# A hybrid decoder step on one core: a fixed expert in the last block, row reads ahead of the last scatter, and a product moved to GpSimd

## The reference

```python
s = sigmoid(h @ w_router)                    # 64 scores, 4 of 8 groups kept
eidx = top_k(masked s + b_router, 8)         # 8 experts of a token
wts = s[eidx] / sum(s[eidx]) * 2.5
routed = sum over the 8 experts e of wts * ((silu(h @ we_g[e]) * (h @ we_u[e])) @ we_d[e])
yf = routed + (silu(h @ ws_g) * (h @ ws_u)) @ ws_d
x = x + gt2 * rms_norm(yf, g_ffn_post)
```

## Time and profile before

| | |
|---|---|
| median of three runs | 1107.8 us (1106.04 to 1108.03) |
| profiled execution | 1108.23 us |
| its span, first to last instruction | 1106.4 us |
| granted TensorE clock, mean | 0.992 |
| busy: TensorE, VectorE, ScalarE, GpSimd | 1065.5, 729.2, 215.3, 136.3 us |
| bytes moved, mean rate | 337.11 MB, 305 GB/s |

### The profile page before, as it was taken

The page is one execution under the profiler, slowest core; times in us unless marked ns, Lnnn a source line. Parts: engine busy times, 40 slices in busy tenths (PEclk is TensorE's granted clock), DMA queues, the critical chain, the costliest instruction groups (busy, mean ns, idle before and its releaser), DMA issues.

```text
span 1106.4 us, 16559 instructions
## 1 busy us (share of the span) xinstructions
PE 1065.5 (96%) x5954; PEld 535.9 (48%) x5954; DVE 729.2 (66%) x1934; ACT 215.3 (19%) x473; POOL 136.3 (12%) x163
## 2 busy tenths in 40 slices
PE   6999999999999999999999999999899999999797
PEld 3456678777877644664333333333233333333242
DVE  3218441546546645766988888888687987888148
ACT  4131332222233313301111111111011110111111
POOL 0110000000020010111121211111112111121100
PEclk9999999999999999999999999999999999999999
DMA  9958720120352277769999999999999999999798
GB/s 368 339 197 301 244 81 24 53 86 1 115 190 87 77 242 248 293 283 380 409 413 425 424 425 424 422 424 427 422 425 424 423 424 420 412 416 406 255 425 334
DMA packets 51653, 337.11 MB, mean 305 GB/s; under 512 B 9636, under 2 KB 14088, under 8 KB 30830
## 3 DMA queue, kind: packets, MB, share of 16 engines
q1 hardware_dynamic: 33710, 287.32, 64.2%
q0 software_dynamic: 17856, 48.68, 11.6%
HBM read 311.30 MB, written 37.24 MB: 315 GB/s over the span
## 4 chain that ended last, share of the span: by engine, by line
PE 79%; DMA 12%; DVE 5%; ACT 2%; issue 1%; SPq 0%; DVEq 0%; ACTq 0%
PE bank L1594 23%; PE bank L1617 12%; PE bank L1289 10%; DMA mem<-in_w_exp_down 6%; PE bank L1308 5%; PE bank L1407 3%; DMA hT<-in_w_exp_down 3%; PE bank L1408 3%; PE bank L1525 3%; PE bank L1202 3%; PE bank L1286 3%; DMA mem<-in_w_sh_down 2%; PE bank L1703 2%; PE bank L1177 1%; DVE mem L2290 1%
## 5 line engine op out<-in xcount | busy, mean ns | idle before, releaser
L1594 PE MATMUL bank<-mem 128*32 128x512 f32 (+2 forms) x1568 | 334.0, 595 | 1.8 <-DVE mem L2290 1.0
L2290 DVE STREAM_TRANSPOSE mem<-mem 32x256 f32<-32x256 f32 x448 | 195.1, 436 | 5.8
L1617 PE MATMUL bank<-mem 128*32 128x512 f32 (+2 forms) x712 | 178.4, 608 | 10.9 <-DMA mem<-in_w_exp_down 7.0
L1594 PEld LDWEIGHTS bank<-mem 128*32 128x32 f32 (+2 forms) x1568 | 106.9, 128 | 164.9 <-issue 164.9
L1289 PE MATMUL bank<-hT,mem 128*128 128x288 f32 x512 | 133.3, 409 | 1.0 <-ACT mem L968 1.0
L2290 DVE STREAM_TRANSPOSE mem<-x_sb 32x256 f32<-32x256 f32 x240 | 104.5, 435 | 3.1
L1289 PEld LDWEIGHTS bank<-hT,mem 128*128 128x128 f32 x512 | 93.8, 190 | 25.8 <-issue 2.4
L1617 PEld LDWEIGHTS bank<-mem 128*32 128x32 f32 (+2 forms) x712 | 56.8, 133 | 81.4 <-issue 71.1
L1594 PE MATMUL bank<-x_sb,mem 128*32 128x512 f32 (+2 forms) x256 | 87.1, 596 | 0.0
L2306 DVE COPY hT<-bank 128x512 f32<-128x512 f32 x48 | 33.1, 691 | 67.2 <-PE bank L1617 67.1
L822 POOL DMA_INDIRECT mem<-ffn_in_rows,idxg x32 | 32.9, 1030 | 268.0 <-DVE idxs L2274 192.6
(11 more groups left out here) (404 smaller groups left out, 1218.9 us busy)
## 6 DMA issues: line engine op xcount, KB each, us to landing
mem<-k_w_exp SPq DMA_DIRECT2D x54, 2048.0 KB
mem<-in_w_exp_down SPq DMA_DIRECT2D x52, 1024.0 KB
x_sb<-k_w_exp SPq DMA_DIRECT2D x10, 2048.0 KB
mem<-k_w_ada SPq DMA_DIRECT2D x8, 2048.0 KB, 9.2
mem<-k_w_in SPq DMA_DIRECT2D x7, 2048.0 KB, 9.0
hT<-in_w_exp_down SPq DMA_DIRECT2D x12, 1024.0 KB
mem<-expert_out_rows SPq DMA_DIRECT2D x6, 2048.0 KB, 15.7
mem<-k_w_head SPq DMA_DIRECT2D x4, 2048.0 KB, 17.3
```

The source lines that it names most:

```text
L1594: i = mm(bank[sl, :], xT[:, j % 2, c * BLK + sl.start:c * BLK + sl.stop], gu_view(r)[:, c, :], start=c == 0, stop=c == KC - 1)
L1617: i = mm(ps[4 + hf][sl, :], hhT[:, k * BLK + sl.start:k * BLK + sl.stop], dn_view(r)[:, k, hf * 512:(hf + 1) * 512], start=k == 0, stop=k ...
L2290: i = dve.transpose(cols[dl, :, sl], rows[sl, :, dl])
```

## The change

Three things are changed together.

1. Expert 63 always takes rank 63, and rank 63 has a block of its own, the last one (capacity 128 rows). `CAPS` is in another order for it, of the same 48 blocks, and the fourth preloaded expert goes to rank 24 instead of 5. Expert 63 is the highest number, so its rows are slot 7 alone; slots 0 to 6 are complete once the scatter before the last has landed.
2. SyncE loads the shared down weights ahead of the x rows. Once the last gate-up product is done and all scatters but the last have landed, it reads the sample tile's slots 0 to 3 and slots 0 to 3 of token tiles 0 and 1 (buffers 0, 1 and 3). The sample tile's slots 4 to 7 and the rest follow the last scatter. Row sets are renumbered, as the sample tile is one set now, and a buffer is free again when VectorE and, for the first set of a tile, TensorE have used it.
3. TensorE adds three instead of four rows of tiles 0, 1 and 2, VectorE five instead of four. The product with the weight row moves to GpSimd for all tiles but the last, and VectorE waits for it (`pch`). VectorE's order becomes own_sum 0, own_sum 1, add_sums 0, residual 0, add_sums 1, then for each further tile own_sum, the residual of the tile before, add_sums.

In the overflow path, which does not run here, the early sets are read a second time.

```diff
-PRE = [0, 1, 4, 5]
+PRE = [0, 1, 4, 24]
+CAPS = [4, 4, 2, 2, 4, 3, 2, 3, 3, 5, 2, 2, 3, 3, 6, 2, 2, 4, 2, 2,
+        4, 2, 2, 5, 4, 3, 4, 4, 4, 2, 2, 3, 1, 3, 5, 3, 1, 3, 3, 3, 3, 5, 6, 1, 4, 4, 4, 2,
+        2, 3, 3, 3, 3, 4, 2, 2, 2, 3, 3, 2, 2, 2, 2, 4]
...
-        COMBINE = [(NCH, KPE)] + [(t, KPE) for t in range(NCH - 1)] + [(NCH - 1, KPE // 2)]
+        COMBINE = [(NCH, KPE)] + [(t, KPE - 1) for t in range(NCH - 1)] + [(NCH - 1, KPE // 2)]
...
+            sp.wait_ge(S["eup"], last_use(EXTSLOT) + 1)
+            load_down(sp, dn_s, A["w_sh_down"][0], S["ld_br"])
             sp.wait_ge(S["eup"], last_use(XSLOT) + 1)
             sp.wait_ge(S["xT_ready"], NBK)
             for t in range(NT):
                 sp.dma_start(x_sb[0:ROWS[t], t, :], x1_d[t * P:t * P + ROWS[t], :]).then_inc(S[f"ld_x{t}"], 16)
-            sp.wait_ge(S["eup"], last_use(EXTSLOT) + 1)
-            load_down(sp, dn_s, A["w_sh_down"][0], S["ld_br"])
+            EARLY = [1, 3]
+            sp.wait_ge(S["eup"], NBK)
+            sp.wait_ge(S["sct0"], 16 * (NBK // 2))
+            sp.wait_ge(S["sct1"], 16 * (NBK // 2 - 1))
+            y_sample(0, "yh0")
+            for q in EARLY:
+                y_rows(q, COMBINE[(q + 1) // 2][0], 0, KPE, f"yh{q}")
...
             for k in range(2):
                 sp.wait_ge(S[f"sct{k}"], 16 * (NBK // 2))
-            for k in range(2):
-                sp.dma_start(yhalf[k:P:2, 0, :], yv[SEQ:T, KPE * k * D:KPE * (k + 1) * D]).then_inc(S[f"yh{k}"], 16)
+            y_sample(1, "yh6")
...
+                    if q >= NYH:
+                        sp.wait_ge(S["yd_sum"], (q - NYH + 1) // 2 + 1)
+                        if (q - NYH) % 2:
+                            sp.wait_ge(S["yp_mm"], (q - NYH + 1) // 2 + 1)
...
+            for i in range(LAST):
+                t = COMBINE[i][0]
+                n = ROWS[t]
+                pool.wait_ge(S["yl_sum"], i + 1)
+                if i:
+                    pool.wait_ge(S["x2_done"], i)
+                pool.tensor_tensor(tgain[0:n], yo[0:n, i % 2, :], bcG[0:n, int(t == NCH), :], ALU.mult).then_inc(S["pch"], 1)
...
-                    y = rows(q, n, 0, KPE)
+                    dve.wait_ge(S[f"yh{(q - 1) % NYH}"], ycount(q - 1))
+                    y = rows(q - 1, n, kp, KPE) + rows(q, n, 0, KPE)
...
-                tt_(tgain[0:n], yo[0:n, i % 2, :], bcG[0:n, o, :], ALU.mult)
+                if i < LAST:
+                    dve.wait_ge(S["pch"], 3 + i)
+                else:
+                    tt_(tgain[0:n], yo[0:n, i % 2, :], bcG[0:n, o, :], ALU.mult)
...
-            for i in range(NT):
+            own_sum(0)
+            own_sum(1)
+            add_sums(0)
+            residual(0)
+            add_sums(1)
+            for i in range(2, NT):
                 own_sum(i)
+                if i < LAST:
+                    residual(i - 1)
                 add_sums(i)
-                if i != LAST - 1:
-                    residual(i)
+            residual(LAST)
```

More of the change, by code:

```diff
@@ L73 @@
 LASTB = [max(b for b in range(NBK) if any(s[2] == r for s in SEGS[b])) for r in range(len(CAPS))]
-RANK = [PRE.index(r) if r in PRE else 0 for r in range(len(CAPS))]
-for i_, r_ in enumerate(sorted((r for r in range(len(CAPS)) if r not in PRE), key=lambda r: -CAPS[r])):
+RANK = [PRE.index(r) if r in PRE else 0 for r in range(len(CAPS) - 1)] + [len(CAPS) - 1]
+assert LASTB.count(NBK - 1) == 1 and CAPS[-1] * QS == BLK
+for i_, r_ in enumerate(sorted((r for r in range(len(CAPS) - 1) if r not in PRE), key=lambda r: -CAPS[r])):
     RANK[r_] = len(PRE) + i_
@@ L680, in _, with y_rows, y_sample @@
                 sp.dma_start(x_sb[0:ROWS[t], t, :], x1_d[t * P:t * P + ROWS[t], :]).then_inc(S[f"ld_x{t}"], 16)
-            sp.wait_ge(S["eup"], last_use(EXTSLOT) + 1)
-            load_down(sp, dn_s, A["w_sh_down"][0], S["ld_br"])
+            yv = y_d.rearrange("(t k) d -> t (k d)", k=TOPK)
+            def y_rows(q, t, k0, k1, s):
+                at_ = (k0 - (q + 1) % 2 * KPE) * D
+                sp.dma_start(yhalf[0:ROWS[t], q % NYH, at_:at_ + (k1 - k0) * D], yv[t * P:t * P + ROWS[t], k0 * D:k1 * D]).then_inc(S[s], 16)
+            def y_sample(k, s):
+                sp.dma_start(yhalf[k:P:2, 0, :], yv[SEQ:T, KPE * k * D:KPE * (k + 1) * D]).then_inc(S[s], 16)
+            EARLY = [1, 3]
+            assert DN_PLACE[NE - 1] not in (1, 3)
+            sp.wait_ge(S["eup"], NBK)
[4 more added lines that the diff above has]
+                y_rows(q, COMBINE[(q + 1) // 2][0], 0, KPE, f"yh{q}")
             nov = overflow_count(sp)
@@ L691, in body, with early_landed @@
                 load_dn(NE + j, e)
+            def early_landed():
+                for q in [0] + EARLY:
+                    sp.wait_ge(S[f"yh{q}"], 16)
             def last_rows():
@@ L697, in last_rows @@
                 sp.sem_inc(S["over"], 1)
-            overflow(sp, nov, body, last=last_rows)
+                y_sample(0, "ld_br")
+                for q in EARLY:
+                    y_rows(q, COMBINE[(q + 1) // 2][0], 0, KPE, "ld_br")
+            overflow(sp, nov, body, early_landed, last_rows)
             sp.wait_ge(S["xT_ready"], NBK)
@@ L721, in _ @@
                         y_rows(q, t, KPE // 2, KPE, f"yh{q % NYH}")
[L722 to L724 removed]
+            y_rows(2 * LAST, t, KPE, TOPK - 2, f"yh{2 * LAST % NYH}")
+            y_rows(2 * LAST, t, TOPK - 2, TOPK - 1, "yh5")
+            y_rows(2 * LAST, t, TOPK - 1, TOPK, "yh6")
             for i, (t, _) in enumerate(COMBINE):
@@ L1712, in _ @@
                 t, kp = COMBINE[o]
-                n, q = ROWS[t], 2 * o
+                n, q = ROWS[t], 2 * o - 1
                 if o < LAST:
@@ L2350, in first_blocks, with last_read @@
                 idx_out(NBK + 1, NBK + 1)
-            overflow(dve, nov, body, first_blocks)
+            def last_read():
+                dve.wait_ge(S["ld_br"], 16 * 4)
+            overflow(dve, nov, body, first_blocks, last_read)
             dve.wait_ge(S["ld_bc"], 4 * SPREAD + 16)
@@ L2363, in own_sum @@
                     tt_(pairs, ident[:, 0:P:2], ident[:, 1:P:2], ALU.add)
-                    for k in range(2):
-                        dve.wait_ge(S[f"yh{k}"], ycount(k))
+                    dve.wait_ge(S["yh0"], 16)
+                    dve.wait_ge(S["yh6"], 16)
                     total, y = yo[:, 0, :], rows(0, P, 0, KPE)
@@ L2372, in own_sum @@
                     dve.wait_ge(S["x2_done"], i - 1)
-                q = 2 * i + 1
+                q = 2 * i
                 if i < LAST:
+                    dve.wait_ge(S[f"yh{(q - 1) % NYH}"], ycount(q - 1))
                     dve.wait_ge(S[f"yh{q % NYH}"], ycount(q))
-                    y = rows(q, n, 0, KPE)
+                    y = rows(q - 1, n, kp, KPE) + rows(q, n, 0, KPE)
                     step(tt_(total, y[0], y[1], ALU.add))
-                    step(tt_(total, total, y[2], ALU.add))
-                    tt_(total, total, y[3], ALU.add).then_inc(S["yd_sum"], 1)
+                    for k in range(2, len(y) - 1):
+                        step(tt_(total, total, y[k], ALU.add))
+                    tt_(total, total, y[-1], ALU.add).then_inc(S["yd_sum"], 1)
                     return
@@ L2459, in shape_constants @@
     e = np.arange(NE)
-    first = np.where(e < len(PRE), (len(PRE) - e) * 2 ** 17, 0)
+    first = np.where(e < len(PRE), (len(PRE) - e) * 2 ** 17, 0) - np.where(e == NE - 1, 2 ** 17, 0)
     k["order"] = np.tile(np.stack([NE - 1 - e + first, np.array(RANK), QS * np.array(CAPS)])[None], (P, 1, 1)).astype(f)
```

19 lines of the change are left out of this document (6 added, 13 removed).

## The result

The changed kernel takes 1116.89 us (median of four runs, 1115.42 to 1117.54), the kernel before 1106.92 in the runs beside it. The ratio is 1.0092, with an interval of 1.0079 to 1.0104: slower by 10 us. Forecast were 1111.6, in a range of 1105 to 1118: the sign and the range held, but the forecast rise was 3.8 us. One of the ten executions of the kernel with only the shared weights moved ran at a granted clock of 0.76 and took 1371 us; it counts in no median and no ratio here.

A forecast was written before the change was run, and what follows sets the result against it. TensorE and the DMA engines were taken to bound the blocks, VectorE the tail from 1066.63 on. 1108.2 + 3.9 - 0.1 - 0.4 = 1111.6 us; own range 1109 to 1114.5, for 8 in 10 1105 to 1118.

The forecast's parts named there:

- Part 1: Expert blocks: rank 34's down weights land 8.9 us later, 6.4 made up, a slow product adds 1.4: +3.9 us.
- one long wait at block 25: Sign at block 25's down product: one wait of about 4 us, and the blocks' end about 4 us later.
- slow product: In the blocks, behind the wait for rank 34's weights: one product at a slow clock, adding 1.4 us.
- Part 2: Tail start: TensorE begins the shared products about 1043.7, ends 7 us earlier, but VectorE's rows now are late.
- Part 3: Tail: the sample's second half queues behind all early rows; VectorE's chain starts at 1066.1 against 1066.63: -0.5 us.
- the sum 1043.4 + 2.9 + 15.0: Sample rows reaching VectorE: issue at 1043.4, 2.9 fixed, 15.0 for 6.4 MB, so 1061.3, not 1056.8.
- Part 4: VectorE's tail chain: four products leave, three adds come, 0.8 of waiting for GpSimd; 34.4 us against 34.0: +0.4.
- (a): Tail: GpSimd's products and VectorE's adds of two buffers exclude each other: +5.1, so 1116.7; chance 0.30.
- The first three are hidden: VectorE's tail chain: three GpSimd products cost nothing, one beside ScalarE's 2.8 us, two beside a 5.0 us sum.
- the gaps between adds: Sign in VectorE's tail sums: gaps of 2 us between adds would be (a); adds at 1.26 throughout deny it.
- the length of a product: GpSimd in the tail: 1.9 us a product, between 0.97 for a memset and 2.9 for three streams.

The follow-up runs named there:

- memset kernel: The changed kernel with GpSimd's product replaced by a memset of the same tile, which only writes: one time of 1111.74 us.

## Why the prediction came out wrong in size

**Part 1, the capacities: mechanism right, size too large.** Forecast +3.9 with bounds of 1 and 6, measured +1.4 us by the ratio of the times, +1.0 by T in that kernel's trace and +0.14 in the trace of after. The one long wait at block 25 came (6.02 and 5.80 us; forecast 3.9, as the early waits it covers were smaller). The landing was 6.75 us late instead of 8.9, for the reason above. From there to T the new order needed 241.09 us against 246.82 before, 5.7 less; forecast were 6.4 less and 1.4 for a slow product, so 5.0. In the profile of after the same terms are 5.65 and 5.51, hence T + 0.14. That trace is the luckiest of eight; on average T is 2 us later with this order than without it.

**Part 2, the shared weights: no effect, as the sum had it, but by a wrong mechanism.** The step took the releaser in the row at its word. With the load long done TensorE stood nearly as long as before. In the changed kernel it began at T + 6.23, not 4.46, in part at the low clock, and was done 3.6 us earlier against T, not 7. It was hidden, as forecast: VectorE never waited for TensorE. Afterwards it idled 7.15 us, and the next four records took 3.67 us instead of 1.93, at a granted clock of 0.57 and 0.75 in the two windows around them:

```profile
1065.00:1070.00 5.00, 1.65 (x2) 0.52 (x3) 3.78 (x4) 0.00 (x0) 0.00 (x0) 0.57 1.03 439
1070.00:1075.00 5.00, 5.00 (x10) 1.80 (x9) 4.90 (x6) 0.00 (x0) 0.00 (x0) 0.75 1.02 436
```

**Part 3, the early reads: the queue was right, two of its terms too small.** That the sample's second half queues behind the early sets was the argument, and the three kernels with other sets confirm it. But the chain was to start at T + 26.9, 0.5 earlier than before, and started at T + 30.07. The step that failed is the sum 1043.4 + 2.9 + 15.0. Of the 3.2 us missing, 1.6 are the issue: T + 5.79 instead of 4.16, as the scatter of block 46 was issued at 1039.65 and SyncE was released 5.5 us later, not 4. The other 1.6 are the transfers. The forecast gave them 426 GB/s from the first byte on; the first ten us showed less:

```profile
1045.00:1050.00 5.00, 4.39 (x7) 1.39 (x8) 0.22 (x1) 0.00 (x0) 0.63 (x1) 0.66 0.84 274
1050.00:1055.00 5.00, 5.00 (x12) 2.01 (x11) 0.00 (x0) 0.00 (x0) 0.00 (x0) 1.00 0.96 365
```

Most of it falls where the last scatter runs beside the reads: the first half of the sample (1.05 MB) landed 6.0 us after its issue, against 5.2 to 5.5 in the kernels that read it behind the scatter, and the first set of 2.1 MB 5.9 us behind it, where sets otherwise landed 4.7 to 5.0 us apart. No run has the early reads without the scatter beside them.

**Part 4, VectorE's chain: the sum held, and rival (a) came on top.** The forecast gave 33.9 us for a GpSimd operation of 0.97 us that hinders nobody. The memset kernel is that case, with 0.95, and has 33.78. So the counting of VectorE's steps was right to 0.1 us. What failed is the overlap: "The first three are hidden: one by ScalarE's 2.8, two by a 5.0 us sum." The first was hidden, the next two were not, as VectorE's add stood still while GpSimd read; this is the largest of the missed terms. It showed not as the gaps between adds that the forecast named as its sign, but as one add of 3.26 us. The chain was 39.62, 5.2 more than the 34.4 of the forecast, and (a) had priced the exclusion at 5.1 with a product of 1.9. The traces give the bill: from the 33.78 of the memset kernel, two pairs of adds 2.04 longer each, and 2.38 us of waiting ahead of tile 2's update where the memset kernel has 0.60. 33.78 + 4.08 + 1.78 = 39.64, measured 39.62. The Trainium skill, "SBUF — State Buffer", section "Who interferes with whom", says that a VectorE operation with two SBUF inputs contends with a GpSimd operation that reads SBUF, not with one that only writes it. The traces agree in both halves: 4.52 and 3.20 against 2.48. The forecast gave (a) 0.30, because no row of the kernel before could show it; but no row there spoke against it either, and the place had the very operands that the page names.

For the length of a product the forecast took 1.9 us. Measured are 2.34 on 64 rows without company, and 3.26 beside an add less the 1.05 us that this add of 1081.22 still had to run, 2.2. The Trainium skill, "GPSIMD Engine Reference", section "3.1 Elementwise — side-by-side cycle accounting", led to an estimate of 2.25; the traces agree within 0.1.

**The account.** Forecast 1111.6; the blocks 3.8 less (T + 0.14), the late start 3.2 more, the chain 5.2 more. The forecast took 0.4 off to get from the profiled execution to the median; the median of after lies 0.2 above its profiled execution instead. 1111.6 - 3.8 + 3.2 + 5.2 + 0.6 = 1116.8, measured 1116.89. Two errors of opposite sign hid each other in part: had the blocks cost the forecast 3.9, the time would have been near 1120.6, outside the range. So that the range held is in part luck. (a) gave 1116.7 from +3.9 for the blocks and +5.1 for the lock, so it met the time by luck too: its block term was as wrong as the forecast's, and the late start was not in it.

**Where the time is,** in profiled tails: the five-row sums with the new order of VectorE and the new last block, not taken apart, +2.5 (69.66 against 67.16), the early sets in front of the needed half +2.7 (72.35), GpSimd's product +3.1 (75.42), and T +0.1. That is the 8.4 us between the two profiled spans. The medians are 10 us apart: the profiled execution of before was itself 1.3 above its median, and that of after 0.2 below.

**What was wrong in the reading of before.** "So the tail is VectorE's, and the transfers run beside it" left out how near the transfers were. With the capacities alone VectorE's chain began 3.3 us earlier on the old tail, and the tail was 67.64 against 67.16 us: both limits lie close together. There neither a faster VectorE nor an earlier start alone can bring much.

## What to carry to other kernels

Work moved from VectorE to GpSimd was free here only where VectorE stood idle. Beside adds of two SBUF buffers the two took turns wherever GpSimd read SBUF, and the bill was nearly the whole length of the GpSimd operation, which for the product is twice VectorE's. Of reads brought forward on one queue, ask first what is then behind them: if the consumer goes in order and its first piece can't be brought forward too, each early byte delays it. When an order of loads is changed, work out again how far the queue has got by then; don't carry the old landing times over. And compare a stage over several traces before calling its cost nothing: here its end moved by 2 us between kernels with the same blocks.

## What the runs showed of the hardware that was not expected

- A row's releaser can name a transfer that does not matter: with the shared weights issued 16 us ahead of T, TensorE's stop ahead of its first product behind the blocks was 4.58 us, against 4.71 with the transfer named as its end. In the eight kernels with the new capacities it was 1.33 to 3.03 us.
- GpSimd on 1024 float32 columns: memset 0.95 us, copy 1.03, product 2.34 without company; beside VectorE's adds 0.95, 1.97 and 3.26. The recorded length of a GpSimd operation includes the time in which it is kept waiting.
- VectorE's waiting shows neither as idle time nor as a releaser: the pair of adds is simply recorded as 4.52 instead of 2.48 us. Only the duration tells of it: one add is recorded as 3.26 us and the next as its usual 1.23.
